# Prompt attention in turns of two query tiles instead of one

## The reference

```python
# NSA: selection and window branch, with 8 blocks of 64 all positions up to the query are seen by both
s = einsum('btkgd,btkmd->btkgm', qr, ks) * scale
p = masked_softmax(s, smask)                 # maximum, exp, sum, quotient, by query row
o_slc = einsum('btkgm,btkmd->btkgd', p, vs)  # o_win likewise, from kw and vw
return g[..., 0:1]*o_cmp + g[..., 1:2]*o_slc + g[..., 2:3]*o_win
# DSA: the same with one branch, whose mask keeps the 128 best keys of each query
```

## Time and profile before

| | us |
|---|---|
| median of 3 runs | 2544.56 (2543.56 to 2545.28) |
| the profiled execution | 2541.22 |
| its span | 2539.5 |
| TensorE busy | 2351.2 (93%) |
| VectorE busy | 1109.2 (44%) |
| ScalarE busy | 712.6 (28%) |
| GpSimd busy | 285.3 (11%) |
| stretch of the NSA prompt attention, 689 to 836 | 147 |
| stretch of the DSA prompt attention, 1956 to 2036 | 80 |

### The profile page before, as it was taken

The page is one execution under the profiler, slowest core; times in us unless marked ns, Lnnn a source line. Parts: engine busy times, 40 slices in busy tenths (PEclk is TensorE's granted clock), DMA queues, the critical chain, the costliest instruction groups (busy, mean ns, idle before and its releaser), DMA issues. The chain is left out here.

```text
span 2539.5 us, 43612 instructions
## 1 busy us (share of the span) xinstructions
PE 2351.2 (93%) x17356; PEld 2121.0 (84%) x17356; DVE 1109.2 (44%) x1802; ACT 712.6 (28%) x1179; POOL 285.3 (11%) x356
## 2 busy tenths in 40 slices
PE   6999999988799889999999999999964989999997
PEld 5999998766644689999998999997742468999997
DVE  5433433222477435434434433433277744443434
ACT  2221222222255123222223222222241513222220
POOL 1000002000255120000020000011040412000002
PEclk8999999997899999999999999999976989999998
DMA  3332332225300222332332332332201012332331
GB/s 101 91 102 81 91 102 65 82 63 182 117 18 1 67 67 83 95 96 86 96 91 75 91 100 83 91 100 67 79 28 56 12 29 80 91 102 81 91 102 56
DMA packets 327479, 202.44 MB, mean 80 GB/s; under 512 B 11698, under 2 KB 306666, under 8 KB 327322
## 3 DMA queue, kind: packets, MB, share of 16 engines
q1 hardware_dynamic: 323226, 199.10, 26.6%
q10 hardware_dynamic: 4160, 2.10, 0.3%
HBM read 194.65 MB, written 10.70 MB: 81 GB/s over the span
## 5 line engine op out<-in xcount | busy, mean ns | idle before, releaser
L156 DVE TENSOR_TENSOR w_lo<-w_stage,w_hi 128x1024 fp32r<-128x1024 f32 (+1 forms) x266 | 350.9, 1319 | 850.2 <-ACT w_hi L149 850.2
L149 ACT ACTIVATE w_hi<-w_stage 128x1024 fp32r<-128x1024 f32 (+1 forms) x266 | 301.9, 1135 | 761.5 <-PE y_ps L163 371.2
L161 PE MATMUL gate_ps<-h_hi,w_hi 128*128 128x260 f32 x1408 | 404.2, 287 | 27.0 <-DVE h_lo L184 19.7
L163 PE MATMUL gate_ps<-h_hi,w_lo 128*128 128x260 f32 x1408 | 402.8, 286 | 0.0
L162 PE MATMUL gate_ps<-h_lo,w_hi 128*128 128x260 f32 x1408 | 401.7, 285 | 0.0
L161 PE MATMUL up_ps<-h_hi,w_hi 128*128 128x260 f32 x1408 | 398.2, 283 | 0.0
L161 PE MATMUL y_ps<-a_hi,w_hi 128*128 128x260 f32 x1408 | 397.9, 283 | 0.0
L163 PE MATMUL up_ps<-h_hi,w_lo 128*128 128x260 f32 x1408 | 397.8, 283 | 0.0
L163 PE MATMUL y_ps<-a_hi,w_lo 128*128 128x260 f32 x1408 | 397.5, 282 | 0.0
L162 PE MATMUL y_ps<-a_lo,w_hi 128*128 128x260 f32 x1408 | 397.4, 282 | 0.0
L162 PE MATMUL up_ps<-h_lo,w_hi 128*128 128x260 f32 x1408 | 396.4, 282 | 0.0
(11 more groups left out here) (425 smaller groups left out, 3246.0 us busy)
## 6 DMA issues: line engine op xcount, KB each, us to landing
w_stage<-w_ffn_in SPq DMA_DIRECT2D x176, 512.0 KB, 3.8
w_stage<-w_ffn_out SPq DMA_DIRECT2D x64, 704.0 KB, 4.5
w_stage<-w_nsa_in SPq DMA_DIRECT2D x20, 512.0 KB, 3.5
w_stage<-w_dsa_in SPq DMA_DIRECT2D x16, 512.0 KB, 3.6
w_stage<-w_nsa_out SPq DMA_DIRECT2D x8, 512.0 KB, 3.5
cmp_page<-cache_nsa_cmp SPq DMA_DIRECT2D x16, 256.0 KB, 3.9
nsa_win_rows<-state_nsa_win SPq DMA_DIRECT2D x16, 256.0 KB, 3.7
w_stage<-w_dsa_out SPq DMA_DIRECT2D x8, 512.0 KB, 3.7
```

The costliest lines, as they stand in the source:

```text
L149: act.activation(e.w_hi[slot][:, 0:cols], e.w_stage[slot][:, 0:cols], ACT.Copy).then_inc(e.hi_done, 1)
L156: dve.tensor_tensor(e.w_lo[slot][:, 0:cols], e.w_stage[slot][:, 0:cols], e.w_hi[slot][:, 0:cols].bitcast(F32), ALU.subtract).then_inc(e.lo ...
L161: pe.matmul(out, w_hi, x_hi, start=first, stop=False)
L163: return pe.matmul(out, w_lo, x_hi, start=False, stop=last)
```

## The change

The three loops take steps of two tiles. In a turn at m (even), TensorE does the scores of tiles m + 2 and m + 3, then the transposes of tiles m - 1 and m, then value products: in the turn at i = 2 the compressed ones and kc = 0 of stage s - 1, in the turn at i = 0 kc = 1, 3, 2 of stage s - 2. ScalarE does two exps, then in the turn at i = 2 the copy of tile 1 and the output. VectorE does weigh(m), maximum(m + 2), weigh(m + 1), maximum(m + 3), then the copies. Buffers, semaphores, their counts and all single operations stay as they are.

```diff
@@ TensorE @@
-            for m in range(M + 1):
+            for m in range(0, M + 1, 2):
                 s, i = m // 4, m % 4
                 if m + 2 < M:
                     scores(m + 2)
+                    scores(m + 3)
                 if m >= 1:
                     turn(m - 1)
-                if m >= 5:
-                    if i == 1 and (s - 1) % nb == 0 and compressed is not None:
+                if m < M:
+                    turn(m)
+                if i == 2 and s >= 1:
+                    if (s - 1) % nb == 0 and compressed is not None:
                         compressed_values(s - 1)
-                    if i == 2:
-                        values(s - 1, 0)
-                    if i == 3:
-                        values(s - 1, 1)
-                        values(s - 1, 3)
+                    values(s - 1, 0)
                 if i == 0 and s >= 2:
-                    values(s - 2, 2)
+                    for kc in (1, 3, 2):
+                        values(s - 2, kc)
@@ ScalarE @@
-            for m in range(M + 1):
+            for m in range(0, M + 1, 2):
                 s, i = m // 4, m % 4
                 if m + 2 < M:
                     exp(m + 2)
+                    exp(m + 3)
                 if i == 2:
                     copy(s)
-                if i == 1 and s >= 2 and (s - 1) % nb == 0:
-                    output((s - 1) // nb - 1)
+                    if s >= 2 and (s - 1) % nb == 0:
+                        output((s - 1) // nb - 1)
@@ VectorE @@
-            for m in range(M + 1):
+            for m in range(0, M + 1, 2):
                 s, i = m // 4, m % 4
                 if m < M:
                     weigh(m)
                 if m + 2 < M:
                     maximum(m + 2)
-                if m >= 1 and i != 2:
+                if m < M:
+                    weigh(m + 1)
+                if m + 2 < M:
+                    maximum(m + 3)
+                if i == 0 and m >= 1:
                     copy(m - 1)
-                if i == 1 and s >= 2 and (s - 1) % nb == 0:
+                if m < M:
+                    copy(m)
+                if i == 2 and s >= 2 and (s - 1) % nb == 0:
                     output((s - 1) // nb - 1)
```

## The result

The changed kernel takes 2591.95 us (median of 4 runs, 2590.58 to 2593.49), the kernel before 2544.76 in the same series. The ratio is 1.0186, with a 95% interval of 1.0169 to 1.0204: slower by 43 to 52 us, 47.2 by the medians. The profiled execution took 2590.58 us, its span is 2588.8.

A forecast was written before the change was run, and what follows sets the result against it. TensorE was taken to bound the kernel, so two added waits per stage lengthen it: NSA 37.6 plus DSA 13.2 is 50.8 us, on the profiled 2541.22 making 2592.0, plus 3.3 for the runs' median: 2595; own range 2585 to 2612.

The forecast's parts named there:

- The waits: Each stage: TensorE waits 1.41 us for VectorE's copy of bank 0 and 1.54 us for ScalarE's of bank 1.
- First turn: Turn at i = 0, from tile 2's scores: 6.27 us, including 1.41 us of wait for VectorE's copy.
- second turn: Turn at i = 2, from tile 0's scores: 5.12 us, including 1.54 us of wait for ScalarE's copy.
- The stages: NSA 11.39 us against 8.90, with the compressed product 12.25 against 9.65; DSA 12.03 against 10.24.
- The sum over each block: Attention stages and ends added up: NSA 37.6 us longer, DSA 13.2, together 50.8.
- The ends: NSA's first stage +1.75 us, second +1.4, last +1.45; DSA's last +0.6, its first two taken as full.
- What was costed at nothing: VectorE's copy of tile 0 (at about 6.4 us), GpSimd's scaling and the moved outputs: taken as covered, no added time.
- The clock: Attention stages: clock stays at 2.4 GHz with TensorE about 74% busy; rival, clock falls, 2646 us, chance 0.10.
- One wait only: Attention stages: only one bank's copy costs, the other comes in time; about +20 us, 2565; chance 0.10.
- The faster rival: Attention stages: copies are out before transposes ask, so stages cost TensorE's pieces alone; some -16 us, 2529; chance 0.04.

The follow-up runs named there:

- TensorE's old order: Against the changed kernel: TensorE's loop is that of the kernel before, VectorE's and ScalarE's stay as changed; 2672.7 us, ratio 1.0512 to before.
- VectorE's copy first: Against the changed kernel: VectorE copies the earlier tile 3 ahead of the maximum of the new tile 3; 2586.5 us, ratio 1.0164 to before.
- TensorE's new order alone: Against the changed kernel: VectorE's and ScalarE's loops are those of the kernel before, one tile each turn; 2571.43 us, ratio 1.0106 to before.

## Why the prediction was right

The forecast was 2595 (+50.8 us by its sum); measured are 2592 and +47.2. Its own range, 2585 to 2612, is 3 us wider on each side than its terms give (7 us down, 14 up).

- *The waits.* First turn: 6.27 us predicted, 6.21 measured (759.38 to 765.59); second turn 5.12 and 5.20. Its 1.41 of wait is 1.28 from the stream's end (762.49 to 763.77), 0.13 less, since VectorE's copy begins 0.08 ahead of the reduce's recorded end, and TensorE follows 0.09 and not 0.14 behind. The second turn's is 1.54 predicted; 766.98 and seven transposes give 767.73, to 769.31 are 1.58.
- *The stages.* 11.39 and 12.25 predicted, 11.41 and 12.27 measured; DSA 12.03 and 12.05.
- *The sum over each block.* NSA from its first score product to the first product of the next block: 689.22 to 844.97 before, 690.87 to 884.76 after, +38.1 against 37.6. DSA likewise: 1956.4 to 2047.6 before, 1994.3 to 2098.8 after, +13.2 against 13.2.
- *The ends*, where that agreement is luck. Counted from one tile 3's score products to the next, the 13 full stages of NSA grew by 33.0 us and five of DSA by 9.1, as summed (33.0, 9.0). The first two distances grew by 2.1 in each block, where the sum has 3.2 and 3.6, and what follows the last tile 3's scores by 3.0 and 2.1, where it has 1.45 and 0.6. One cause can be read: the value products kc = 1, 3, 2 of the last stage but one, 1.44 us, now come behind the last score products. The sum took them off NSA's second stage, and its 1.45 for the last stage is hardly more than the first wait's 1.41.

```profile
866.62 1.13 PE L889 MATMUL nsa_att_s_ps<-nsa_kt,nsa_qt 64*128 64x512 f32 x4
...
870.31 1.52 PE L940 MATMUL nsa_att_o_ps<-nsa_att_pt,nsa_z 128*64 128x384 f32 x12
```

- *The missing 2 to 4 us* lie outside: the attention blocks account for 51.4 us of a profile that grew by 49.3. One place can be read: the block after NSA's attention started at a clock of 0.91 before (847 to 857) and 1.00 after (884 to 895), its first group of products taking 1.76 us and 1.14. I take this as chance in where the clock stands, which a sum over the change cannot hold; from the first product behind NSA's attention to DSA's first score product, where no edit reaches, the eleven profiles have 1109.2 to 1113.5 us.
- *What was costed at nothing.* VectorE's copy of tile 0 comes at 765.70 for a turn that began at 759.38, 6.32, where 6.4 was said; the next maximum starts 766.33, 0.32 after its mask, so it is not late. GpSimd shows one wait of 0.9 us, in NSA's last stage, which the prediction did not name; it is part of the 3.0 us above.
- *The clock* stayed at 1.00 with TensorE busy 78% (145.86 of 186). In TensorE's old order, with waits of 1.78 and 1.98 us, it was 0.88 and 0.83. The Trainium skill ("TensorE: Matmul & The Clock Gate", section "A second HAM failure mode: psum-queue depth-cycling") tells of a kernel whose frequent short idles between groups of matmuls made the clock swing. The changed kernel's trace does not show it (1.00 throughout, with two idles a stage); the old order's looks like it, at 0.88 and 0.83.
- *The rivals.* "One wait only" would have been 2565: covering just the first gives 2570, and taking most of the second 2571.5, so the two waits share the loss nearly evenly. The faster rival, pieces alone, gave 2529; with both waits for copies covered 2535 to 2538 was reached. It missed the 0.23 us a stage that covering costs, and a stage at 8.78 has another 0.1 whose cause I did not look for.

## What to carry to other kernels

Before grouping the steps of two tiles on each engine, look at the buffers between the engines. Here the banks were still two: count, for each bank, what the consumer has queued ahead of the read-out and what the producer has to do meanwhile. Whether four banks would make the grouping pay was not run. If the producer is the full engine, put its independent work between the two fillings (48 us here). Letting the consumer read out first gained 20 us on ScalarE and 5 on VectorE, where the late maximum took part of it back. Before regrouping, look where rare work (here an output once a stage) stands in a helper engine's order: moving it one turn gave 8 us, as much as the whole regrouping done well, which holds that move too. A change that regroups loops moves such work along with the rest, so time that move by itself.

## What the runs showed of the hardware

- The busy share alone doesn't tell whether TensorE keeps its clock: 78% busy with waits of 1.10 and 1.39 us (by the brackets) kept 1.00, and 75% busy (180.77 of 240, at the lower clock for part of it) with waits of 1.98 and 1.78 us had 0.88 and 0.83. The old order's run took about 38 us more than the sum made at 2.4 GHz. That the longer waits did it is argued: no run changed the waits' length alone.
- A single longer wait was followed by groups at half speed in five places: VectorE's copy first, 1.60 us in NSA and in DSA; TensorE's new order alone, 1.72 us in NSA's second stage and 1.48 and 1.63 us in the last stages. In DSA's second stage of that run a wait of 1.72 us was not, with the clock at 1.00. So the length of one wait doesn't tell it either.
- Gains from two waits add up in a full stage and not in the kernel's time: 0.97 and 0.53 us a stage alone gave 1.37 together, but 20 us and 5 us alone gave 20.5 together, because the blocks' second and last stages got longer by waits for exps and GpSimd, most of them followed by groups at half speed in the profile.
